# Eighteen of 22 up-projection chunks as seven block products instead of eight, with the hi/lo splits of the gated values moved to the down projection

## What is computed

```python
f_gate, f_val = jnp.split(x @ w_up, 2, axis=-1)          # x (544, 1024), w_up (1024, 2 * 2816)
ffn_ext = jnp.concatenate([ffn_hist, f_gate], axis=1)    # two frames of history
f = jax.nn.gelu(causal_dwconv(ffn_ext, ffn_conv_w, ffn_conv_b), approximate=False) * f_val   # width 3
x = layer_norm(DN_ALPHA * x + f @ w_down, ln2_g, ln2_b)  # w_down (2816, 1024)
```

## Time and profile before

| what | value |
|---|---|
| median of 3 runs | 1798.47 us (1798.11 to 1800.48) |
| span of the profiled execution | 1796.6 us, so 1.9 us of the median lie around the span |
| PE busy | 1783.3 us (99%), 14234 matmul records |
| DVE busy | 1141.6 us (64%) |
| ACT busy | 773.2 us (43%) |
| POOL busy | 101.0 us (6%) |
| granted TensorE clock | 0.998 of full speed |
| moved by DMA | 186.00 MB, mean 104 GB/s |

### The profile page before, as it was taken

The page is one execution under the profiler, slowest core; times in us unless marked ns, Lnnn a source line. Parts: engine busy times, 40 slices in busy tenths (PEclk is TensorE's granted clock), DMA queues, the critical chain, the costliest instruction groups (busy, mean ns, idle before and its releaser), DMA issues.

```text
span 1796.6 us, 32671 instructions
## 1 busy us (share of the span) xinstructions
PE 1783.3 (99%) x14234; PEld 1749.4 (97%) x14234; DVE 1141.6 (64%) x1745; ACT 773.2 (43%) x1260; POOL 101.0 (6%) x159
## 2 busy tenths in 40 slices
PE   9999999999999999999999999999999999999997
PEld 9998999999999999999999989999999999999997
DVE  5798787755764444446668886786558644445565
ACT  4256533353453344434542564324535534444343
POOL 0025100000100000000000350000001000000000
PEclk9999999999999999999999999999999999999999
DMA  4522122223222222255525221222222222222544
GB/s 172 170 96 72 54 78 83 94 72 116 96 71 82 84 95 95 68 177 181 170 92 169 74 93 38 83 94 78 99 106 71 92 74 94 94 85 94 182 165 137
DMA packets 36511, 186.00 MB, mean 104 GB/s; under 512 B 7376, under 2 KB 11728, under 8 KB 18192
## 3 DMA queue, kind: packets, MB, share of 16 engines
q1 hardware_dynamic: 34672, 176.28, 29.0%
q10 hardware_dynamic: 1696, 7.64, 1.2%
HBM read 176.75 MB, written 7.15 MB: 102 GB/s over the span
## 4 chain that ended last, share of the span: by engine, by line
PE 96%; DVE 3%; issue 1%; DMA 0%; ACT 0%; ACTq 0%; DVEq 0%
PE acc L1685 29%; PE acc L1690 29%; PE acc L1691 29%; PE score L1761 1%; PE small L1812 1%; PE turned L1792 1%; DVE acc L1202 1%; PE score L1690 1%; PE score L1691 1%; PE score L1685 1%; PE turned L1854 1%; PE score L1978 0%; DMA raw<-win 0%; PE small L1827 0%; PE score L1771 0%
## 5 line engine op out<-in xcount | busy, mean ns | idle before, releaser
L1685 PE MATMUL acc<-xh,wh 128*128 128x272 f32 x2944 | 857.0, 291 | 1.5 <-DVE xl L952 1.3
L1690 PE MATMUL acc<-xl,wh 128*128 128x272 f32 x2944 | 847.5, 288 | 0.0
L1691 PE MATMUL acc<-xh,wl 128*128 128x272 f32 x2944 | 847.1, 288 | 0.0
L1685 PEld LDWEIGHTS acc<-xh,wh 128*128 128x128 f32 x2944 | 554.4, 188 | 9.1 <-issue 5.7
L1690 PEld LDWEIGHTS acc<-xl,wh 128*128 128x128 f32 x2944 | 554.2, 188 | 0.1
L1691 PEld LDWEIGHTS acc<-xh,wl 128*128 128x128 f32 x2944 | 553.0, 188 | 0.0
L998 DVE TENSOR_TENSOR wl<-raw,wh 128x2048 fp32r<-128x2048 f32 (+2 forms) x154 | 318.4, 2068 | 215.6 <-ACT wh L505 215.0
L505 ACT ACTIVATE wh<-raw 128x2048 fp32r<-128x2048 f32 (+2 forms) x174 | 305.2, 1754 | 180.5 <-DMA raw<-wdn 132.7
L1685 PE MATMUL acc<-fhh,wh 128*128 128x272 f32 x704 | 204.1, 290 | 0.0
L1691 PE MATMUL acc<-fhh,wl 128*128 128x272 f32 x704 | 202.7, 288 | 0.0
L1690 PE MATMUL acc<-fll,wh 128*128 128x272 f32 x704 | 202.3, 287 | 0.0
(11 more groups left out here) (268 smaller groups left out, 2279.2 us busy)
## 6 DMA issues: line engine op xcount, KB each, us to landing
raw<-win SPq DMA_DIRECT2D x50, 1024.0 KB, 4.9
raw<-wup SPq DMA_DIRECT2D x44, 1024.0 KB, 4.9
raw<-wdn SPq DMA_DIRECT2D x32, 1024.0 KB, 4.9
raw<-wbr SPq DMA_DIRECT2D x24, 512.0 KB, 3.6
raw<-wdn SPq DMA_DIRECT2D x16, 768.0 KB, 4.2
raw<-wout SPq DMA_DIRECT2D x8, 1024.0 KB, 4.9
v_out<-vfm ACTq DMA_DIRECT2D x2, 1088.0 KB, 8.7
k_out<-k ACTq DMA_DIRECT2D x2, 1088.0 KB, 4.9
```

The costliest lines, as they stand in the source:

```text
L1685: first = mm(out, a, xs[0], start=start, stop=False)
L1690: mm(out, a, xs[1], start=False, stop=False)
L1691: return mm(out, b, xs[0], start=False, stop=stop)
```

## The change

For 18 of the 22 chunks (nine gate/value pairs, i = 2 to 10; here called quads, q = 0 to 17, even ones gate and odd ones value), the weights of a chunk are seen as 2x2 blocks: output tile m by half of K. The activations are seen as 2x2 blocks too: half of K by half of the frames. The 2x2 block product is made with seven products of 4 K tiles instead of eight (Winograd's form). With A for weights and x for activations:

- POOL forms, once a layer, the four differences of the activations `traw[T1..T4N]` (128x1088 each), and for each quad three sums of weight blocks into `sraw` and one that replaces a block in `raw` (four tensor_tensor of 128x512, function `sums`).
- ACT and DVE split those sums too (`shi`, `slo`), beside the chunk itself, which is now split in halves (`second_blocks`, `first_blocks`, `first_low`, `other_lows`).
- PE issues the products P1 to P7 of a quad in that order, 12 matmuls each. P1, P3, P5 and P6 accumulate in one bank (PB). What the bank holds after P1, P3 and P5 is copied by ACT into `m1`, `u1`, `u3` (`snapshot`); P2 goes to PA; P4 and P7 to PC, into which P7 is only added after DVE has read it (`bottom_right`).
- DVE adds the snapshots to the banks (`bottom_right`, `left`), ACT copies the fourth block (`top_right`). Gate blocks go to `gex`, value blocks in float32 to `f32`, where `gated_values` multiplies them in place.
- The hi/lo splits of f now happen in six groups of tiles for each half, at the end of the up stage and in the down stage (`f_his`, `f_lows`).

Line 482's use of POOL, the ring of three slots and the loads stay as they are. The core of the diff:

```diff
+QUADS = 18
+PRODUCTS = 7
+
+ORDER = []
+for _q in range(QUADS):
+    ORDER += [(_q, _p + 1) for _p in range(PRODUCTS)]
...
+for _q in range(QUADS + 1):
+    ACT_ORDER += [("u3", _q - 1)] if _q else []
+    ACT_ORDER += [("m1", _q)] if _q < QUADS else []
+    ACT_ORDER += [("c12", _q - 1)] if _q else []
+    ACT_ORDER += [("u1", _q)] if _q < QUADS else []
...
+                def sums(q):
...
+                    pool.wait_ge(raw_full[s], 16 * (SLOT[:j + 1].count(s) - (1 if s < 2 else 0)))
+                    if q > 1:
+                        pool.wait_ge(prod_full, full_at(r, q - 2, 5))
+                    g.tensor_tensor(s1, a21, a22, ALU.add).then_inc(s_made, 1)
+                    pool.wait_ge(s_made, made + 1)
+                    g.tensor_tensor(a21, a11, a21, ALU.subtract).then_inc(s_made, 1)
+                    g.tensor_tensor(s2, s1, a11, ALU.subtract).then_inc(s_made, 1)
+                    pool.wait_ge(s_made, made + 3)
+                    if q > 1:
+                        pool.wait_ge(prod_full, full_at(r, q - 2, 6))
+                    g.tensor_tensor(s4, a12, s2, ALU.subtract).then_inc(s_made, 1)
...
+                for q in range(QUADS + 1):
+                    if q:
+                        snapshot("u3", q - 1, 5, "c22")
+                    second_blocks(q + 1)
+                    if q < QUADS:
+                        snapshot("m1", q, 1, "c11")
...
+                    if q and q % 2 == 0:
+                        conv_gelu(0)
+                    if q:
+                        top_right(q - 1)
+                    first_blocks(q + 1)
+                    if q and q % 2 == 0:
+                        conv_gelu(1)
+                    two_sums(q + 1)
+                    last_sum(q + 1)
...
+                    if q < QUADS:
+                        snapshot("u1", q, 3, "c21")
+                    if q % 2:
+                        first_tap(q - 1)
...
+                for q in range(QUADS + 1):
+                    if q:
+                        bottom_right(q - 1)
+                    if q and q % 2 == 0:
+                        conv_close(1 + q // 2, (1,), False)
+                    if q < QUADS:
+                        left(q, 0)
+                    first_low(q + 1)
+                    if q:
+                        left(q - 1, 1)
+                    if q and q % 2 == 0:
+                        gated_values(q - 1)
...
+                    other_lows(q + 1)
+                    if q % 2:
+                        history(2 + q // 2)
+                        conv_close(2 + q // 2, (0,), False)
+                    if q == QUADS - 1:
+                        f_lows(0, 0)
+                for g_ in range(1, 3):
+                    f_lows(0, g_)
+                lo()
+                for g_ in range(3, 6):
+                    f_lows(0, g_)
...
+                    if p == 5:
+                        pe.wait_ge(snapped, act_at(r, "u1", q))
+                    if p == 6:
+                        pe.wait_ge(snapped, act_at(r, "u3", q))
+                        pe.wait_ge(s_ready, sums + 2)
+                    if p == 7:
+                        pe.wait_ge(combined, dve_at(r, "c22", q))
```

More of the change, by code:

```diff
@@ L135, in trunk @@
         xT = sb("xT", [P, KT, T])
+        XAT = top[0]
         xh = sb("xh", [P, KT, T], F32R)
@@ L881, in conv_open, with turned_x_hi @@
                         A(cbuf[:, m, :], cbuf[:, m, :], ACT.Gelu).then_inc(fgelu_full, c.up(fgelu_full))
[L883 to L886, removed]
+                def turned_x_hi():
+                    for n, j in enumerate((T1, T3, T2, T4N)):
+                        act.wait_ge(t_made, 4 * l + n + 1)
+                        A(th[j][:, :, :], traw[j][:, :, :], ACT.Copy).then_inc(t_hi, 1)
@@ L1580, in f_products, with f_lows @@
                                                      ALU.mult).then_inc(acc_free[b], c.up(acc_free[b]))
[L1582 to L1587, removed]
+                def f_lows(h, g):
+                    a, b = FGROUPS[g]
+                    dve.wait_ge(f_hi, c.take(f_hi))
+                    v.tensor_tensor(fll[h][:, a:b, :], f32[h][:, a:b, :], fhh[h][:, a:b, :].bitcast(F32),
+                                    ALU.subtract).then_inc(f_ready, c.up(f_ready))
@@ new lines, in other_lows @@
+                def other_lows(q):
+                    if q < QUADS:
+                        s, n = SLOT[turn[0] - 1], CHUNK // 2
+                        dve.wait_ge(s_made, 4 * (l * QUADS + q) + 4)
+                        v.tensor_tensor(wl[s][:, n:], raw[s][:, n:], wh[s][:, n:].bitcast(F32), ALU.subtract).then_inc(
+                            lo_full[s], c.up(lo_full[s]))
+                        i = q % 2
+                        for n, part in enumerate((slice(0, 2), slice(2, 3))):
+                            dve.wait_ge(s_hi, 2 * (l * QUADS + q) + n + 1)
+                            v.tensor_tensor(slo[i][:, part, :], sraw[i][:, part, :], shi[i][:, part, :].bitcast(F32),
+                                            ALU.subtract).then_inc(s_ready, 1)
@@ new lines, in bottom_right @@
+                def bottom_right(q):
+                    i, bank, u3 = 2 + q // 2, PC[q % 2], snap[q % 2]["u3"]
+                    dve.wait_ge(prod_full, full_at(l, q, 5))
+                    dve.wait_ge(snapped, act_at(l, "u3", q))
+                    if q % 2 == 0:
+                        v.tensor_tensor(gex[:, 1, 2 + HALF:2 + SEQ], bank[:, 0:BP], u3[:, 0:BP], ALU.add)
+                        v.tensor_tensor(gex[:, 1, 4 + SEQ:GEX], bank[:, BP:HALF], u3[:, BP:HALF], ALU.add).then_inc(combined, 1)
+                    else:
+                        v.tensor_tensor(f32[1][:, 2 * i + 1, :], bank[:, 0:HALF], u3[:, :], ALU.add).then_inc(combined, 1)
@@ new lines, in left @@
+                def left(q, m):
+                    i = 2 + q // 2
+                    bank, add = (PA[q % 2], snap[q % 2]["m1"]) if m == 0 else (PC[q % 2], snap[q % 2]["u1"])
+                    dve.wait_ge(prod_full, full_at(l, q, 7 if m else 2))
+                    dve.wait_ge(snapped, act_at(l, "u1" if m else "m1", q))
+                    out = gex[:, m, 2:2 + HALF] if q % 2 == 0 else f32[0][:, 2 * i + m, :]
+                    v.tensor_tensor(out, bank[:, 0:HALF], add[:, :], ALU.add).then_inc(combined, 1)
@@ L1613, in _ @@
                 shift_sum(0)
-                los(3)
+                for g_ in range(3, 6):
+                    f_lows(1, g_)
+                    los(1)
                 centre(0)
@@ L2046, in down @@
+                for n in range(len(ORDER)):
+                    products(n)
+                pe.wait_ge(combined, dve_at(r, "c11", QUADS - 1))
                 def down(h, middle=None):
```

290 lines of the change are left out of this document (245 added, 45 removed).

## The result

| what | before | after |
|---|---|---|
| median | 1798.36 us (1798.11 to 1800.48) | 1904.01 us (1902.21 to 1907.61) |
| span of the profiled execution | 1796.6 us | 1900.8 us |
| PE, DVE, ACT, POOL busy | 99, 64, 43, 6% | 94, 70, 44, 18% |
| granted TensorE clock | 0.998 | 0.977 |

The change makes the kernel slower: ratio 1.0589, 95% interval 1.0574 to 1.0604, 105.7 us. The forecast was 1842 us, at most 1884. The sign was right, the size was not: +106 us where +43 stood.

A forecast was written before the change was run, and what follows sets the result against it. The prediction took PE as the bound, busy 96% of the span. Per layer, waits exceeded savings by 19.3 us, plus 2.3 at the down stage: +43.2 us over two layers, 1842 us; forecast range 1825 to 1860, 8 in 10 1797 to 1884.

The forecast's parts named there:

- P6 of even quads: PE waits before P6 while ACT copies the bank it shares with P5: 0.83 us in each quad.
- P6 of odd quads: The same wait for ACT's copy between P5 and P6, put at 0.83 us with ACT taken as free.
- P7 of odd quads: PE waits before P7 for DVE's addition, behind taps that alternate with POOL's sums: 2.36 us.
- the walk: Step-by-step timing of a quad pair, POOL and two-input DVE instructions taking turns: 26.65 us a pair instead of 24.07.
- the rival put on the tail copies: Two-element DVE copies between taps each wait one POOL sum: 1.3 us at odd quads' P7, +21 us, 1863; chance 0.14.
- I take nothing: The two-element DVE copies between the taps were costed at no delay from POOL.
- P7 of even quads: PE waits before P7 for DVE's addition, behind a split that waits for POOL's first sum: 1.12 us.
- the rival in which DVE goes first: A DVE instruction next in line passes a waiting POOL, so even quads' 1.12 us goes: -18 us, 1824; chance 0.15.
- The head: Start of the up stage: POOL's four activation differences and their splits, covered by 30 us of PE work, cost nothing.
- The clock: Waits might lower PE's granted clock; half speed in one quad in ten would add 38 us; chance 0.07.
- The start of the down stage: PE waits for DVE's split of the second weight chunk: 2.3 us a layer; later chunks covered.
- The rival without turns: POOL's sums hardly delay DVE, so P7 waits shrink or vanish: 1796, or 1779 on its faster side; chance 0.19.

The follow-up runs named there:

- The first experiment: On the changed kernel, DVE makes the history copies of odd quads ahead of the next quad's lo parts instead of behind them; 1912.68 us, ratio 1.0633.
- the two runs with constants: POOL's four sums a quad became constant writes: on the changed kernel 1858.39 us; on it with history copies first and tail copies on ACT 1808.09 us.

## Why the prediction was right and wrong

- **PE's saving** (1.505 us a quad, 54.2 in all): right, 432 records fewer at an unchanged 0.125 us.
- **P6 of even quads**, 0.83: measured 0.65 + 0.10. PE's start followed the end of the copy by 0.05 instead of 0.15 us (621.95 + 0.40 to 622.40).
- **P6 of odd quads: the step that failed.** "ACT's copy ends at 0.44" took ACT to be free. I followed PE and DVE through the odd quad, but not what ACT waits for just ahead of `u3`: `first_tap` waits for DVE's `history`, which stands behind `other_lows` and, as an instruction that takes turns, behind POOL's first sum. 3.70 us, 24.1 us a layer more than forecast. The first experiment shows the cause. The order stood in the lists printed ahead of the prediction, where L1764 is a row between `other_lows` and the tap; that `first_tap` waits for it (`gex_full`) stands in the kernel.
- **P7 of odd quads**, 2.36: it did not show, since P6 was late by more: 1.3 us a layer instead of 18.9, which takes back most of the 24.1. With P6 mended it was 3.40, with the tail copies elsewhere 2.17, within 0.2 of the walk. So the walk by turns was right and was hidden, and the 1.3 us that the rival put on the tail copies were 1.23 where they could show.
- **"I take nothing" for the two-element copies: wrong.** They take turns: 1.24 us for one of them against 0.15 for its twin (609.09 and 610.24). I had chosen the value by the one-input reciprocal; the row that was nearer to it in kind, a copy beside POOL, was not in the trace. The Trainium skill, SBUF — State Buffer, in its section on SBUF's two separate sides, says that a float32 SBUF copy takes the shared pair as a two-input op does; the copies of this case agree with it.
- **P7 of even quads**, 1.12: measured 1.27. POOL's turn of 2.21 us (622.06) in the middle of DVE's two splits of 2.91 is the picture that the walk drew; POOL got its turn between the two, against the rival in which DVE goes first. That POOL and DVE exclude each other in turns is borne out by the two runs with constants.
- **P5**, 0.45: 0.20 + 0.10.
- **The head, "I cost them at nothing": wrong**, 7.4 us in one layer and 6.0 in the other, within the bound of 11 that I gave if the cover were gone. The cover of 30 us of PE's work was there, but the three engines' lists put the copies and products that PE waits for behind that work.
- **The clock: left out of the sum, and a rival at 0.07.** It fell behind 18 of the 20 waits of 2.7 to 3.8 us, and the slow steps sum to 31.9 us, near the rival's 38, though a part of them lies where PE would have waited for DVE. Pairs in which it didn't fall take 28.15 us (634.34 to 662.49), those with a short stretch 28.8 to 29.0 and those with a long one 30.0. It was not only the longer wait that did it: with odd quads at 0.65 and 2.17, close to the walk's waits, the kernel took 1877 and not 1842 us, with 20.4 us of slow steps and 13.4 us of waits at the heads.
- **The start of the down stage**, 2.3: 2.26 for the second chunk and 0.91 for a later one, which the forecast had called covered.
- **The rival without turns**, 1796 or 1779: with the order mended and no turns the kernel takes 1808, with 0.65 us at each P6 and the waits at the head and in the down stage left, so this rival's faster side did not show even there.

A pair, forecast at 26.65 us, is 21.1 + 3.70 + 0.65 + 1.27 + 0.20 of waits, and about 0.4 of slow second steps and 1.5 of low clock where it fell for a short stretch: 28.8.

Of the 29.8 us a layer by which the waits and steps exceed the forecast (78.5 against 48.7), P6 and P7 of odd quads together are 6.5, the head is 7.4, and the slow and second steps are 17.7; the rest is -1.8. So the path that I had wrong gives only a fifth of the miss by itself, besides the falls of the clock behind its longer waits. That my forecast of 18.9 us at P7 nearly made up for it is luck.

What stays open: why the clock fell behind some waits and not behind others of the same length, whether POOL's load or its turns weigh more, and whether a deeper interleave of products would hide the rest; no run was made on any of the three alone.

## What to carry to other kernels

Before costing a bank copy that an engine must make between two matmul groups, read that engine's whole list just ahead of it, and for each wait there the list of the engine that releases it: here the wait was two lists away. A form with fewer products pays only if other matmuls stand between the products that share a bank; with one chunk at a time it lost 106 us, with the next chunk's products between them 14, and with the lists set to match it won 15. A late engine that is mended at one wait shows up at the next, so the waits of one stage are mended together or not at all. And a wait on PE can need a second price beside its own length, for the matmuls behind it: here 1.3 to 2.7 us each time that the clock fell, behind waits of 2.2 to 3.8 us.

## What the runs showed of the hardware

- A DVE copy of 128x2 elements waits for its turn as a large two-input instruction does: 1.22 us beside a POOL sum of 128x512, and at the head of the stage beside a POOL difference of 128x1088 even 2.5 us. Changed kernel, DVE and then POOL:

```profile
523.78 2.50 DVE L1753 COPY fst<-gex 128x2 f32<-128x2 f32 x1
```

```profile
520.73 5.53 POOL L553 TENSOR_TENSOR traw<-xT,traw 128x1088 f32<-128x1088 f32 x2
```

- POOL's write of a constant (0.52 us for 128x512) left DVE's splits and taps at their own 0.683 and 0.79 us. The history copies beside it were longer, 0.389 us in the median of all 44 against 0.156 at the shortest: the small copy was held where the two-input instruction was not. No run was made on this alone.
- Behind 18 of the changed kernel's 20 waits of 2.7 to 3.8 us the granted clock was 0.50, and 11 to 26 matmuls came 0.226 us apart instead of 0.125 (1.3 to 2.7 us lost each time); behind the two others (638.17 and 754.20) it was 1.00. With waits of 2.17 us (tails on ACT) it fell in 8 of 16 odd quads. After the changed kernel's waits of 0.5 to 1.1 us no such stretch was seen.
- A wait costs PE more than the profile's idle figure: 0.49 idle is 0.65 lost to the first start (621.63 to 622.40), and 0.10 more to the second.
